# q and k transposed by DMA on 16-bit halves instead of on TensorE, with B's rotations spread to unit 14 and the exponentials ahead of a unit's weight split

## The reference

```python
for l in range(DEPTH):                      # DEPTH = 2
    h = rms_norm(x, norm_mix[l])
    z = h @ w_in[l]                         # 1024 -> 6656 columns, 13 chunks of 512
    qa, ka, va, qb, kb, vb, uc, gz = jnp.split(z, SPLIT_POINTS, axis=-1)
    qa = apply_axial_rope(rms_norm(qa.reshape(b, s, 8, 64), qn_a[l]), ang_row, ang_col)
    ka = apply_axial_rope(rms_norm(ka.reshape(b, s, 2, 64), kn_a[l]), ang_row, ang_col)
    ya = dense_gqa_blocked(qa, ka, va) @ w_branch_a[l]
    qb = apply_rope(rms_norm(qb.reshape(b, s, 12, 64), qn_b[l]), ang_seq)
    kb = apply_rope(rms_norm(kb.reshape(b, s, 12, 64), kn_b[l]), ang_seq)
    ...                                     # three head groups, dilated windows, weights from the denominators
    yc = multiscale_pool(uc, pool_lin[l], pool_scale[l]) @ w_branch_c[l]
    gates = sigmoid(gz + b_gate[l]).reshape(b, s, 3, 1024)
    x = x + (gates[:, :, 0] * ya + gates[:, :, 1] * yb + gates[:, :, 2] * yc) @ w_out[l]
    h2 = rms_norm(x, norm_ffn[l])
    x = x + (silu(h2 @ w_ffn_gate[l]) * (h2 @ w_ffn_up[l])) @ w_ffn_down[l]
```

## Time and profile before

| | |
|---|---|
| median of three runs | 838.54 us (838.47 to 838.91) |
| the profiled execution: its time | 838.81 us |
| its span, first to last instruction | 837.0 us |
| PE busy | 830.0 us, 99% |
| DVE busy | 562.2 us, 67% |
| ACT busy | 422.8 us, 51% |
| POOL busy | 178.0 us, 21% |
| granted TensorE clock | 1.000 |

### The profile page before, as it was taken

The page is one execution under the profiler, slowest core; times in us unless marked ns, Lnnn a source line. Parts: engine busy times, 40 slices in busy tenths (PEclk is TensorE's granted clock), DMA queues, the critical chain, the costliest instruction groups (busy, mean ns, idle before and its releaser), DMA issues.

```text
span 837.0 us, 10043 instructions
## 1 busy us (share of the span) xinstructions
PE 830.0 (99%) x4012; PEld 679.0 (81%) x4012; DVE 562.2 (67%) x688; ACT 422.8 (51%) x505; POOL 178.0 (21%) x174
## 2 busy tenths in 40 slices
PE   8999999999999999999999999999999999999998
PEld 7888778888888888888888877878888888888886
DVE  5998565666875766655379985566586766666552
ACT  6766544464454454443456574553833554544430
POOL 1443000000024444430024320000000443444200
PEclk9999999999999999999999999999999999999999
DMA  9745344435457676775455442443455577767651
GB/s 349 280 163 191 121 152 165 150 134 193 157 196 221 199 221 220 227 236 211 168 189 201 175 170 108 176 153 127 155 195 174 197 226 213 214 209 224 208 202 49
DMA packets 46350, 157.38 MB, mean 188 GB/s; under 512 B 26048, under 2 KB 26208, under 8 KB 28896
## 3 DMA queue, kind: packets, MB, share of 16 engines
q1 hardware_dynamic: 44384, 150.48, 53.3%
q0 software_dynamic: 1632, 6.18, 2.1%
q10 hardware_dynamic: 288, 0.08, 0.0%
HBM read 149.91 MB, written 1.05 MB: 180 GB/s over the span
## 4 chain that ended last, share of the span: by engine, by line
PE 97%; DVE 1%; ACT 1%; DMA 1%; issue 0%; SPq 0%
PE bank L976 30%; PE bank L987 29%; PE bank L978 29%; PE bank L1009 4%; PE bank L1110 2%; PE bank L1086 1%; PE bank L1077 1%; PE bank L1050 1%; DMA x_sb<-in_x_dram 1%; PE bank L1056 0%; DVE w_lo L695 0%; DVE w_lo L701 0%; ACT w_hi L546 0%; ACT zvu L662 0%; DVE scratch L719 0%; ACT aT_hi L556 0%
## 5 line engine op out<-in xcount | busy, mean ns | idle before, releaser
L695 DVE TENSOR_TENSOR w_lo<-w_raw,w_hi 128x2048 fp32r<-128x2048 f32 x134 | 309.7, 2313 | 125.3 <-ACT w_hi L546 125.0
L976 PE MATMUL bank<-w_hi,aT_hi 128*128 128x512 f32 x832 | 330.7, 397 | 0.3 <-issue 0.2
L978 PE MATMUL bank<-w_hi,aT_lo 128*128 128x512 f32 x832 | 324.5, 390 | 0.0
L546 ACT ACTIVATE w_hi<-w_raw 128x2048 fp32r<-128x2048 f32 x134 | 256.3, 1914 | 125.0 <-DMA w_raw<-in_stream_dram 124.7
L987 PE MATMUL bank<-w_lo,aT_hi 128*128 128x512 f32 x832 | 223.5, 390 | 0.1
L976 PEld LDWEIGHTS bank<-w_hi,aT_hi 128*128 128x128 f32 x832 | 156.2, 188 | 36.9 <-issue 4.9
L987 PEld LDWEIGHTS bank<-w_lo,aT_hi 128*128 128x128 f32 x832 | 155.6, 188 | 33.2 <-DVE w_lo L695 0.7
L978 PEld LDWEIGHTS bank<-w_hi,aT_lo 128*128 128x128 f32 x832 | 156.4, 188 | 31.2
L484 POOL COPY halves<-hid 128x512 uint16<-128x512 uint16 x44 | 70.6, 1633 | 4.5 <-DVE hid L948 4.5
L976 PE MATMUL bank<-w_hi,hT_hi 128*128 128x512 f32 x176 | 68.7, 390 | 0.0
L978 PE MATMUL bank<-w_hi,hT_lo 128*128 128x512 f32 x176 | 68.5, 389 | 0.0
(11 more groups left out here) (97 smaller groups left out, 734.1 us busy)
## 6 DMA issues: line engine op xcount, KB each, us to landing
w_raw<-in_stream_dram SPq DMA_DIRECT2D x135, 1024.0 KB, 4.8
bias_sb<-in_b_gate_dram POOLq DMA_DIRECT2D x12, 256.0 KB, 4.5
par<-in_params_dram POOLq DMA_DIRECT2D x3, 384.0 KB, 3.5
w_raw<-in_stream_dram SPq DMA_DIRECT2D x4, 256.0 KB, 5.6
pool_mat<-in_pooling_dram POOLq DMA_DIRECT2D x1, 1024.0 KB, 5.3
out_dram<-x_sb SPq DMA_DIRECT2D x4, 256.0 KB, 4.0
x_sb<-in_x_dram SPq DMA_DIRECT2D x2, 256.0 KB, 4.4
x_sb<-in_x_dram SPq DMA_DIRECT2D x1, 512.0 KB, 6.6
```

Source lines behind the costliest of these rows:

```text
L546: nc.scalar.activation(w_hi[:, j % RING, :, :].rearrange("p k n -> p (k n)"), w_raw[:, j % RING, :, :].rearrange("p k n -> p (k n)"), ACT. ...
L695: nc.vector.tensor_tensor(w[0], w[1], w[2].bitcast(F32), ALU.subtract).then_inc(unit_lo, 1)
L976: nc.tensor.matmul(o, src[0][:, k, tok], w_hi[:, slot, wk + i, :], start=first and i == 0, stop=False)
L978: nc.tensor.matmul(o, src[1][:, k, tok], w_hi[:, slot, wk + i, :], start=False, stop=False)
```

## The change

- REGIONS: the rotations of B's heads move from units 5, 5, 6, 7, 8, 9, 10, 11 to units 5, 6, 7, 8, 10, 12, 14, 14.
- The "qk" turns are gone from TensorE and from ScalarE (nine batches in a layer, 34 transposes and nine copies).
- In the unit after a rotation, at the end of its unit's work, ScalarE splits the normed step of zqk into 16-bit halves (split_heads, twelve in a layer; 1024, 512 or 256 elements wide), into a new tile head_halves that shares its place with tiles used later.
- SyncE, after the load that follows the end of that unit, waits for the split and issues a transposing DMA back into zqk (turn_heads).
- In the units of JOIN_UNITS ScalarE joins the halves into qkT (join_heads, twelve in a layer).
- ScalarE takes a pair's exponentials (softmax_exp) before the split of unit t + 2, where it took them after it.
- GpSimd's norms of the heads stand in a loop over units; their order is the same.

```diff
@@ REGIONS @@
-    ("b_k0", QK_B_K, 8, 22, 3, 3, (8, 9)),
-    ("b_k1", QK_B_K + 8 * HD, 4, 30, 3, 4, (10, 11)),
+    ("b_k0", QK_B_K, 8, 22, 3, 3, (10, 12)),
+    ("b_k1", QK_B_K + 8 * HD, 4, 30, 3, 4, (14, 14)),
+JOIN_UNITS = (8, 8, 10, 12, 16, 17)
-    6: [("qk", 0)], 7: [("qk", 2)], 14: [("qk", 6)],
...
+HEAD_TILES = [(0, 4), (4, 1), (5, 2), (7, 4), (11, 4), (15, 2)]
...
@@ SyncE @@
+            def turn_heads(lay, r, m):
+                sp.wait_ge(heads_split, lay * TURNED + (MT * r + m + 1))
+                sp.dma_start_transpose(turned_room(r, m).rearrange("p (g t) -> p g t", t=P), split_room(r, m)
+                                       ).then_inc(heads_turned[r], 16)
...
+                for n in range(TURNED):
+                    if lay >= 0 and REGIONS[n // MT][-1][n % MT] == t - 1:
+                        turn_heads(lay, *divmod(n, MT))
@@ ScalarE @@
-                elif kind == "qk":
-                    first, k = QK_BATCH[i]
-                    free(nc.scalar.activation(qkT[:, first:first + k, :].rearrange("p k n -> p (k n)"),
-                                              B(name)[:, 0:k * SEQ], ACT.Copy), name)
...
+            def split_heads(lay, n):
+                r, m = divmod(n, MT)
+                first, k = HEAD_TILES[r]
+                act.wait_ge(rotated, lay * TURNED + (n + 1))
+                both = zqk[:, m, P * first:P * (first + k)].bitcast(U16).rearrange("p (f h) -> p h f", h=2)
+                to = split_room(r, m).rearrange("p (h f) -> p h f", h=2)
+                nc.scalar.activation(to, both, ACT.Copy).then_inc(heads_split, 1)
+            def join_heads(lay, r, m):
+                first, k = HEAD_TILES[r]
+                act.wait_ge(heads_turned[r], (lay + 1) * 16 * MT)
+                both = qkT[:, first:first + k, P * m:P * m + P].bitcast(U16).rearrange("p k (t h) -> p h k t", h=2)
+                nc.scalar.activation(both, turned_room(r, m).rearrange("p (h k t) -> p h k t", h=2, t=P),
+                                     ACT.Copy).then_inc(heads_joined, 1)
...
-                    for j in splits_at(t, ahead=3):
-                        split(lay, j)
                     p = pair_at(t, 0)
                     if p is not None:
                         softmax_exp(lay, 2 * p)
                         softmax_exp(lay, 2 * p + 1)
+                    for j in splits_at(t, ahead=3):
+                        split(lay, j)
...
+                    for n in range(TURNED):
+                        if REGIONS[n // MT][-1][n % MT] == t - 1:
+                            split_heads(lay, n)
+                    for r in range(len(REGIONS)):
+                        if JOIN_UNITS[r] == t:
+                            for m in range(MT):
+                                join_heads(lay, r, m)
@@ TensorE, scores @@
                 if p == 0:
-                    wait_emptied(pe, lay, ("qk", 2))
+                    pe.wait_ge(heads_joined, lay * TURNED + 2 * 2)
                 if p == 4:
-                    wait_emptied(pe, lay, ("qk", 7))
-                    wait_emptied(pe, lay, ("qk", 8))
+                    pe.wait_ge(heads_joined, lay * TURNED + TURNED)
```

More of the change, by code:

```diff
@@ L135, in turns_within @@
     return TURNS_WITHIN.get(t, [])
[L139 removed]
+HEAD_TILES = [(0, 4), (4, 1), (5, 2), (7, 4), (11, 4), (15, 2)]
 SCALED = ("mix_x", "mixed", "ffn_x")
 SPLIT = ("o", "merged", "hidden")
[L142 removed]
+PLAIN = ("probs", "pool")
 X_BANKS = (4, 0)
@@ L256, in build @@
         pool_mat = sb("pool_mat", [P, MT, POOL_G, SEQ])
+        with ExitStack() as shared:
+            head_halves = sb("head_halves", [P, 20 * MT * 2 * P], U16, shared)
         mixT_hi = sb("mixT_hi", [P, POOL_G, SEQ], F32R)
@@ L327, in build @@
         hidden_ready = sem("hidden_ready")
+        heads_split = sem("heads_split")
+        heads_turned = [sem(f"heads_turned{r}") for r in range(len(REGIONS))]
+        heads_joined = sem("heads_joined")
         vchain = sem("vchain")
@@ L467, in x_norms, with head_norm @@
                       sx[:, which, :], 1.0 / D, EPS, x_norm)
+            def head_norm(lay, n):
+                (name, _, hs, first, _, _, _), m = REGIONS[n // MT], n % MT
+                mul, eps = (1.0, HD * EPS) if name[2] == "q" else (1.0 / HD, EPS)
+                pool.wait_ge(head_sums, lay * TURNED + (n + 1))
+                h = slice(first, first + hs)
+                power(lay, 2 + n, (rs[:, m, h], rs_in[:, m, h], neg_half[:, m, h]),
+                      ss[:, m, h], mul, eps, head_norms)
             def load_bias(lay, g):
@@ L506, in _ @@
                                    ).then_inc(pooling_loaded, 16)
[L507 to L516, removed]
+                for t in range(U_C0):
+                    for n in range(TURNED):
+                        if REGIONS[n // MT][-1][n % MT] == t:
+                            head_norm(lay, n)
                 for g in range(2, 6):
@@ L1028, in transposes @@
                         last = turn(P * k, merged[:, m, P * (UK * half + k):P * (UK * half + k + 1)])
-                elif kind == "qk":
-                    first, k = QK_BATCH[i]
-                    region = (0, 0, 1, 2, 3, 3, 4, 4, 5)[i]
-                    pe.wait_ge(rotated, lay * TURNED + 2 * (region + 1))
-                    for j in range(k):
-                        for m in range(MT):
-                            last = turn(P * (2 * j + m), zqk[:, m, P * (first + j):P * (first + j + 1)])
                 elif kind == "probs":
```

18 lines of the change are left out of this document (14 added, 4 removed).

## The result

| | median of 5 runs (us) | range | span of the profiled execution | mean granted clock |
|---|---|---|---|---|
| before | 838.84 | 838.47 to 840.32 | 837.0 | 1.00 |
| after | 881.63 | 879.47 to 882.24 | 879.8 | 0.98 |

The ratio is 1.0505, 95% interval 1.049 to 1.0519: the changed kernel is 5% slower. The forecast was 876, its range 851 to 893.

A forecast was written before the change was run, and what follows sets the result against it. The prediction took TensorE, 97% of the chain, to bound the kernel. New waits of 22.9 us per layer, 45.8 for two, less 8.4 removed, gave +37.4 on 838.8: 876 us, range 851 to 893.

The forecast's parts named there:

- the part that decides: Order inside a pair of score banks: rounding and w_lo split enter the chain from maxima to division, 8.21 us, was 4.93.
- Pairs 3 to 7: TensorE waits for the division 1.3 us in pair 3, 0.7 in each later pair, plus 0.3 to 0.9 for banks.
- Pair 0: First score pair of a layer: late maxima make TensorE wait 8.0 us for the division, ready at 86.0, due at 78.1.
- Pair 1: Second score pair: maxima 3.45 us behind the scores, division ready at 11.66, due at 8.11, so TensorE waits 3.6 us.
- rival 3: TensorE's clock falls in the new gaps, costing 2 to 5 us per layer, 884 us; chance 0.12.
- Pair 2: Third score pair: TensorE waits 4.15 us for the division, plus 0.9 for the bank VectorE empties behind it.
- What was removed: The "qk" transposes on TensorE and one bank wait per layer: 8.4 us saved over two layers.
- Order only: The exponentials' order costs, but ScalarE's splits hide in its idle time; pair 0 waits 3.2 us; 855 us, chance 0.15.
- 16-bit activations dear: ScalarE's big 16-bit copies each take 0.86 us longer, by GpSimd's ratio: +6 us per layer, 888 us; chance 0.12.
- The clock falls: TensorE's granted clock drops in the new waits, a unit then taking 10.9 us instead of 5.4; 884 us, chance 0.12.
- The waits stay hidden: No new TensorE wait appears and the 8.4 us removed are gained: 830 us; chance 0.05.
- The DMA path: A join waits for its transposing DMA, seen as ScalarE idle before joins; 880 to 895 us, chance 0.04.

The follow-up runs named there:

- experiment 1: The changed kernel with ScalarE rounding unit t + 2 before the pair's exponentials again, all else as changed; 848.54 us, ratio 1.0121.
- experiment 6: The changed kernel with small extra matmuls keeping TensorE busy ahead of the transposes of pairs 0 and 2; 877.54 us, ratio 1.0466.
- experiment 4: The changed kernel with head splits and their transposing DMAs two units behind the rotation instead of one, last join in unit 18; 868.42 us, ratio 1.036.
- experiment 5: The changed kernel with rounding ahead of the exponentials again and head splits two units behind their rotations; 833.11 us, ratio 0.9937.
- experiment 7: The changed kernel with rounding first, head splits two units behind, B's k rotations in units 9, 11, 12, 13, some joins earlier, joins on GpSimd; 830.98 us, ratio 0.9912.
- experiment 3: The changed kernel with VectorE's division of a pair ahead of its w_lo split of unit t + 2; 862.37 us, ratio 1.0286.
- experiment 2: The kernel before with only the exponentials moved ahead of the rounding of unit t + 2, q and k still transposed on TensorE; 864.20 us, ratio 1.0308.
- experiment 8: The changed kernel with rounding first, head splits two units behind, B's k rotations in units 9, 11, 12, 13, some joins earlier, on ScalarE; 832.11 us, ratio 0.9924.

## Why the prediction came out

**What bounded the kernel, and the part that decides.** As forecast. From maxima to division the forecast had 8.21; it is 8.23 in pair 0 (from 8.34 to 16.57 us behind the scores) and 8.23 to 8.25 in pairs 1 to 3, and experiment 1 puts it back to 4.94 by the order alone. Pairs 3 to 7 cost 6.5 us in a layer, forecast 6.2 with the banks.

**Pair 0, forecast 8.0, measured 11.2: two terms.** With the clock held it is 9.9 in experiment 6, about 9.5 with the overrun of the extra products taken off.
- *The join, mis-sized.* The prediction took 0.95 between big 16-bit copies. The head split has 1.059, as forecast, but the join, which writes every other 16-bit element, has 1.358, and the four joins ahead of unit 11's rounding took 3.10 until it, not 2.5. That rounding started at 66.09 and not 65.1, and everything behind it is 1.0 later, the maxima at 78.8 and not 77.8. The other 0.4 of this 1.0 was there before the joins (w_lo split at 59.10, not 58.7, and the head split behind it). The scores themselves came 0.6 earlier than forecast, at 70.43 and not 71.0, so the maxima stand 8.34 us behind them and not 7. These 1.0 and 0.6 make up the 1.5 between 8.0 and 9.5.
- *The clock.* It was priced as a rival with 0.12; it belonged into the sum, because the forecast's own waits of 8.0 and 4 us are long idle stretches. It costs some 1.8 in pair 0. The forecast's 10.9 us for a unit at the lower level was a little high: at the measured 0.427 from matmul to matmul, 24 of them take 10.2.

The Trainium skill, "ScalarE: Activation LUTs", section "What ACT_TABLE_LOAD costs", gives 186 ns and 0.833 ns per element for an activation with immediate scale and bias, which makes an estimate of 1.04 us for 1024; the head split (1.059) agrees and the join (1.358) does not.

The Trainium skill, "TensorE: Matmul & The Clock Gate", section "What's actually happening", has the clock drop to half when TensorE idles long enough; the rows above now show it, behind 9.20 and 3.67 us.

**Pair 1, forecast 3.6, measured 2.0.** At full clock it is 3.1 in experiment 6, about 3.5 without the overrun, so the term was right. VectorE's path from pair 0's division to pair 1's maxima, forecast 9.5, took 9.42 and does not depend on TensorE: what the clock cost in pair 0 was mostly swallowed here, which rival 3 had said.

**Pair 2, forecast 5.05, measured 6.6.** At full clock it is 20.90 - 15.85 = 5.05, so that term was right and the clock adds 1.6.

**What was removed, forecast 8.4, measured 9.8.** The first layer gives 2.19 + 2.94 = 5.1 and the second 1.75 + 3.1 = 4.9 where the forecast had 4.2 each; the end took 0.2 longer. Whether each removed batch was worth more than its 0.44 or something else went with them was not tried.

**The sum.** 5.6 us too low: 2 x 1.65 for the pairs at full clock (pair 0 +1.5, pair 1 -0.1, pair 2 none, pairs 3 to 7 together +0.25), 2 x 1.8 for the clock (measured in the first layer alone), less 1.4 that went besides: 5.5. That the last term has the other sign is luck. The result is nearer to rival 3's 884 than to the 876 of the sum.

**The rivals.** *Order only* (855) falls with experiment 1: the lateness of pair 0 stays when the order is undone, and goes with experiment 4. *16-bit activations dear* was right in direction for the join alone, at 0.30 us and not 0.86. *The clock falls* came true beside the forecast. *The waits stay hidden* is what experiments 5 and 7 look like, and took both undone: with the chain at 4.94 and the maxima at 2.44, pair 0 is ready 7.38 behind its scores, just in time. *The DMA path* never bound: no idle time before a join in the changed kernel.

## What to carry to other kernels

When an instruction moves ahead of another in one engine's queue, follow what the second one feeds: here 1.8 us of exponentials ahead of a rounding put 3.3 us into a chain on another engine that had had 0.5 to 2 us to spare. Where two engines hand results to each other once per step, add up the ring, and leave a step between giving and taking; that and the old order turned 5% slower into 0.6% faster, and joins on an engine with time to spare, with earlier rotations, into 0.9%. And a forecast that holds long waits must hold what they cost besides: the time around each, and TensorE's clock.

## What the runs showed of the hardware

- ScalarE's copies of 16-bit elements cost more in the join, which writes every other element, than in the head split, which reads every other: 1.358 against 1.059 us for 1024 elements, 0.782 against 0.627 for 512. That the strided output is the reason was not tried by itself.
- TensorE was at 1.2 GHz when it took up work behind idle stretches of 9.20, 5.99, 4.43, 3.89, 3.67 and 3.52 us (the changed kernel and experiments 1, 3 and 4), and stayed at 2.4 GHz behind 1.52 and 2.29 (the changed kernel and experiment 2). Between these both happened: the clock fell 0.9 us behind a wait of 2.43 (experiment 4), 0.7 behind one of 2.72 (experiment 6, second layer) and 1.5 behind one of 3.04 (experiment 2), but not behind one of 2.67 (experiment 6, first layer). Behind 9.20 us of idle time it stayed low for 3.9 us of work, behind 3.67 us for 5.5.
- Eight transposes behind a wait of 1.01 us took 1.29 us to the next matmul, some 0.3 of it for the second bank's division, and 0.79 without a wait.
- In experiment 7 GpSimd's copies of 512 16-bit elements took 0.77 us beside VectorE's maxima. Where one ran at the same time as a w_lo split for the split's whole length it took 2.8, and the split took 2.6 to 2.8 us instead of 2.29. In experiment 8, without these copies, the same splits took 2.29.
